# DSA attention weights left unnormalised, the outputs of a head pair multiplied by transposed reciprocals

## What is computed

```
logits = einsum('bhqd,bqkhd->bhqk', qb, kg) * D_HEAD ** -0.5     # over selected keys
logits = where(sel_ok, logits, -inf)
p = softmax(logits)                                              # exp(l - max) / sum
out = einsum('bhqk,bqkhd->bqhd', p, vg)
```

## Time and profile before

| | |
|---|---|
| median of 3 runs | 1843.07 us |
| profiled execution, own time | 1841.95 us |
| its span | 1840.2 us, mean clock of PE 0.99 |
| PE / PE loads / DVE / ACT / POOL busy, share of the span | 96% / 81% / 56% / 38% / 22% |
| DSA jobs | about 741 to 939 us from the start |
| idle of PE before an instruction, longest in the DSA stage | 4.69 us, for v_raw |

### The profile page before, as it was taken

One profiled execution on the slowest core, in us unless ns is written; L12 is line 12 of the kernel. 1 busy time (PEld: TensorE's weight loads), 2 busy tenths in 40 slices (PEclk: granted clock), 3 DMA queues, 4 the chain that ended last, 5 costly groups with the idle time before them and its releaser, 6 DMA issues. The chain is left out here.

```text
span 1840.2 us, 25612 instructions
## 1 busy us (share of the span) xinstructions
PE 1761.6 (96%) x10056; PEld 1495.7 (81%) x10056; DVE 1023.2 (56%) x1764; ACT 703.2 (38%) x1375; POOL 398.4 (22%) x174
## 2 busy tenths in 40 slices
PE   5999999999999999899999899999999999999998
PEld 4889888899877788788878688888888888888886
DVE  5387888999999997577744254323222222222225
ACT  5366444444444443799932233302111121203032
POOL 1111212321111111111014500404132222314033
PEclk9999999999999999899999899999999999999999
DMA  4564424423423323444134432302020211112023
GB/s 166 162 188 138 130 78 126 143 93 98 111 73 104 101 74 96 113 94 94 42 114 150 161 116 79 92 12 80 12 80 25 68 46 46 57 35 76 17 75 143
DMA packets 65583, 170.54 MB, mean 93 GB/s; under 512 B 9320, under 2 KB 23976, under 8 KB 65464
## 3 DMA queue, kind: packets, MB, share of 16 engines
q1 hardware_dynamic: 65464, 168.91, 30.5%
HBM read 126.47 MB, written 42.41 MB: 92 GB/s over the span
## 5 line engine op out<-in xcount | busy, mean ns | idle before, releaser
L594 PE MATMUL bk<-x_hi,w_hi 128*128 128x512 f32 (+2 forms) x832 | 308.6, 371 | 1.2 <-PEq L284 1.2
L594 PE MATMUL bk<-x_lo,w_hi 128*128 128x512 f32 (+2 forms) x832 | 298.2, 358 | 0.0
L594 PE MATMUL bk<-x_hi,w_lo 128*128 128x512 f32 (+2 forms) x832 | 297.6, 358 | 0.0
L265 POOL TENSOR_TENSOR w_lo<-w_raw,w_hi 128x1024 fp32r<-128x1024 f32 x53 | 131.4, 2480 | 478.1 <-ACT w_hi L261 478.1
L1370 ACT ACTIVATE relu<-bank 128x1024 f32<-128x1024 f32 x32 | 33.0, 1030 | 504.5 <-PE bank L1281 504.5
L1281 PE MATMUL bank<-m_hi,w_hi 128*128 128x512 f32 x512 | 199.5, 390 | 0.0
L1281 PE MATMUL bank<-m_hi,w_lo 128*128 128x512 f32 x512 | 199.2, 389 | 0.0
L1281 PE MATMUL bank<-m_lo,w_hi 128*128 128x512 f32 x512 | 199.2, 389 | 0.0
L935 DVE TENSOR_SCALAR_CACHE_REDUCE sel<-sc,st_bits 128x272 bf16<-128x272 f32 (+6 forms) x217 | 184.2, 890 | 0.9
L1451 DVE TENSOR_TENSOR acc<-acc,bank 128x1024 f32<-128x1024 f32 x56 | 68.4, 1221 | 192.5 <-PE bank L1257 191.6
L594 PEld LDWEIGHTS bk<-x_hi,w_hi 128*128 128x128 f32 x832 | 158.7, 191 | 17.0 <-issue 1.3
(11 more groups left out here) (177 smaller groups left out, 3586.9 us busy)
## 6 DMA issues: line engine op xcount, KB each, us to landing
w_raw<-w_units SPq DMA_DIRECT2D x99, 512.0 KB, 3.8
raw<-w_units SPq DMA_DIRECT2D x24, 512.0 KB, 3.5
k_hi<-k_d SPq DMA_DIRECT2D x32, 260.0 KB, 5.4
k_lo<-k_d SPq DMA_DIRECT2D x32, 260.0 KB, 6.0
q_st<-q_d SPq DMA_DIRECT2D x32, 256.0 KB, 4.6
g_d<-stage_hi SPq DMA_DIRECT2D x32, 256.0 KB
gate<-g_d SPq DMA_DIRECT2D x16, 512.0 KB, 4.4
v_raw<-v_d SPq DMA_DIRECT2D x16, 260.0 KB, 7.2
```

Source lines behind the costliest of these rows:

```text
L265: pool.tensor_tensor(w_lo[:, s], w_raw[:, s], w_hi[:, s].bitcast(F32), ALU.subtract).then_inc(lo_done, 1)
L594: mm = pe.matmul(pj[b][:, 0:c1 - c0], w[:, s, kt, :], a[:, kt, c0:c1], start=kt == 0 and k == 0, stop=kt == KT - 1 and k == 2)
```

## The change

The exponent writes its row sums to one column per job: 16 columns for the 8 blocks of a head pair. `normalise` is gone on ACT and on DVE, and `turn` of a DSA job waits for the exponent. The product is then of unnormalised weights, and ACT copies it to `o_pair` for all four pairs. When the 16 jobs of a pair have their sums, DVE inverts the 16 columns in one instruction, and ACT copies them to `r_wide`, 1024 columns, each reciprocal repeated 64 times: column block 128i + 64(head) is for block i. Eight transposes of 128x128 on PE (`turn_sums`, two groups in the ring of four banks) turn `r_wide` into the layout of `o_pair`: the partition is the head dimension of either head, the column the query. DVE multiplies the pair by the two banks (`scale_pair`), ACT rounds it, POOL makes the rest. For the last pair DVE only copies the banks to `r_last`; multiplication, rounding and rest stand at the start of the branch stage, and PE waits for them at row tile 7 of the first output tile. `sum_col`, `HI_NO` and the tile addresses are bookkeeping.

```diff
+RELOAD = [NJ // 2 + 6 + 10 * p_ for p_ in range(4)]
+PAIR_AT = [NJ // 2 + 16 * (p_ + 1) + 3 for p_ in range(3)] + [NJ + 1]
...
+    if j_ in PAIR_AT:
+        for half_ in range(2):
+            tp_take(("r", PAIR_AT.index(j_), half_), j_)
+R_GROUPS = sorted(n_ for key_, n_ in TPN.items() if key_[0] == "r")
+HI_NO = [n_ - sum(r_ < n_ for r_ in R_GROUPS) for n_ in range(len(TP_BANK))]
...
-        o_pair = at("o_pair", [P, 3, SEQ], F32, O_SC)
+        o_pair = [at(f"o_pair{p}", [P, SEQ], F32, O_SC + 4096 * p if p < 3 else O_STAGE) for p in range(4)]
+        r_wide = at("r_wide", [P, SEQ], F32, O_SC + 3 * 4096)
+        r_last = at("r_last", [P, SEQ], F32, O_STAGE + 4096)
...
+            def sum_col(j):
+                t, g, i = JOBS[j]
+                return 128 + 16 * ((g - H) // 2) + 2 * i + g % 2
...
-                    pe.wait_ge(a_done, j + 1)
+                    if t == SB:
+                        pe.wait_ge(a_done, j + 1)
+                    else:
+                        pe.wait_ge(exp_done, j + 1 - NJ // 2)
...
+                def turn_sums(p):
+                    pe.wait_ge(r_spread, p + 1)
+                    for half in range(2):
+                        n = TPN["r", p, half]
+                        turn_bank(n)
+                        for m in range(4):
+                            i = 4 * half + m
+                            mm = pe.transpose(bk[TP_BANK[n]][:, m * P:(m + 1) * P], r_wide[:, i * P:(i + 1) * P], idf[:])
                         mm.then_inc(tp_ready, 1)
...
+                    if j in PAIR_AT:
+                        turn_sums(PAIR_AT.index(j))
...
-                                   accum_out=small[:, 20 + j % 4:21 + j % 4]).then_inc(exp_done, 1)
-
-                def normalise(j):
-                    keys, s = KEYS[JOBS[j][2]], j % 2
-                    a = a_buf[:, j % 3, 0:keys]
-                    act.wait_ge(recip, j - NJ // 2 + 1)
-                    act.activation(a, a, ACT.Copy, scale=small[:, 24 + s:25 + s]).then_inc(a_done, 1)
+                                   accum_out=small[:, sum_col(j):sum_col(j) + 1]).then_inc(exp_done, 1)
...
-                    elif j < PAIRED:
-                        r = DH * (g % 2)
+                    else:
+                        r, p = DH * (g % 2), (g - H) // 2
                         if j == NJ // 2:
                             act.wait_ge(mask_done, 1)
-                        act.copy(o_pair[r:r + DH, g // 2 - 4, i * P:(i + 1) * P], bk[o_bank(j)][0:DH, 0:P]).then_inc(o_free, 1)
-                    else:
-                        r = DH * (g % 2)
-                        act.copy(o_hi[r:r + DH, g // 2, i * P:(i + 1) * P], bk[o_bank(j)][0:DH, 0:P]).then_inc(oh_done, 1)
+                        if j == NJ // 2 + 48:
+                            act.wait_ge(or_lo, 3)
+                        act.copy(o_pair[p][r:r + DH, i * P:(i + 1) * P], bk[o_bank(j)][0:DH, 0:P]).then_inc(o_free, 1)
...
+                def spread(p):
+                    if p:
+                        act.wait_ge(tp_ready, TPN["r", p - 1, 1] + 1)
+                    act.wait_ge(recip, p + 1)
+                    act.copy(r_wide[:].rearrange("p (c d) -> p c d", d=DH),
+                             small[:, 192 + 16 * p:208 + 16 * p].unsqueeze(2).broadcast_to([P, 16, DH])).then_inc(r_spread, 1)
...
                 def round_pair(p):
-                    act.wait_ge(o_free, STEPS + 16 * (p + 1))
-                    act.copy(o_hi[:, 4 + p, :], o_pair[:, p, :]).then_inc(op_hi, 1)
+                    act.wait_ge(tp_free, TPN["r", p, 1] + 1)
+                    act.copy(o_hi[:, 4 + p, :], o_pair[p][:]).then_inc(op_hi, 1)
...
-                    if 1 <= j < NJ + 1 and JOBS[j - 1][0] == DS:
-                        normalise(j - 1)
...
+                    if j > NJ // 2 and j % 16 == 0:
+                        spread((j - NJ // 2) // 16 - 1)
...
-                def normalise(j):
-                    t, g, i = JOBS[j]
-                    s, e, keys = j % 2, j - NJ // 2, KEYS[i]
-                    dve.wait_ge(exp_done, e + 1)
-                    if e >= 2:
-                        dve.wait_ge(a_done, j - 1)
-                    dve.reciprocal(small[:, 24 + s:25 + s], small[:, 20 + j % 4:21 + j % 4]).then_inc(recip, 1)
+                def reciprocals(p):
+                    dve.wait_ge(exp_done, 16 * (p + 1))
+                    dve.reciprocal(small[:, 192 + 16 * p:208 + 16 * p], small[:, 128 + 16 * p:144 + 16 * p]).then_inc(recip, 1)
...
+                def scale_pair(p):
+                    if p < 3:
+                        dve.wait_ge(o_free, NJ // 2 + 16 * (p + 1))
+                    else:
+                        dve.wait_ge(or_lo, 4)
+                    for half in range(2):
+                        n = TPN["r", p, half]
+                        src, cols = bk[TP_BANK[n]][:], slice(half * HALF, (half + 1) * HALF)
+                        dve.wait_ge(tp_ready, n + 1)
+                        if p < 3:
+                            dve.tensor_tensor(o_pair[p][:, cols], o_pair[p][:, cols], src, ALU.mult).then_inc(tp_free, 1)
+                        else:
+                            dve.tensor_copy(r_last[:, cols], src).then_inc(tp_free, 1)
...
-                def rest_output(j):
-                    t, g, i = JOBS[j]
-                    r = DH * (g % 2)
-                    dst = (slice(r, r + DH), g // 2, slice(i * P, (i + 1) * P))
-                    dve.wait_ge(oh_done, j + 1 - PAIRED)
-                    dve.tensor_tensor(o_lo[dst], bk[o_bank(j)][0:DH, 0:P], o_hi[dst].bitcast(F32), ALU.subtract).then_inc(o_free, 1)
 
...
-                    if 1 <= j < NJ + 1:
-                        if JOBS[j - 1][0] == SB:
-                            stick(j - 1)
-                        else:
-                            normalise(j - 1)
+                    if 1 <= j < NJ + 1 and JOBS[j - 1][0] == SB:
+                        stick(j - 1)
+                    if j > NJ // 2 and j % 16 == 0:
+                        reciprocals((j - NJ // 2) // 16 - 1)
                     if j < NJ and JOBS[j][0] == DS:
                         logits(j)
...
-                    if j - 4 >= PAIRED:
-                        rest_output(j - 4)
...
+                    if j in PAIR_AT:
+                        scale_pair(PAIR_AT.index(j))
...
-                        mm = unit_mm(pe, u % 2, o_hi, o_lo, outs, kts=range(4 * t, 4 * t + 4))
+                        mm = unit_mm(pe, u % 2, o_hi, o_lo, outs, kts=range(4 * t, 4 * t + 4),
+                                     before=lambda kt: pe.wait_ge(last_lo, 1) if k == 0 and kt == KT - 1 else None)
...
+                act.wait_ge(last_mul, 1)
+                act.copy(o_hi[:, KT - 1, :], o_pair[3][:]).then_inc(last_hi, 1)
...
+                dve.tensor_tensor(o_pair[3][:], o_pair[3][:], r_last[:], ALU.mult).then_inc(last_mul, 1)
+                dve.wait_ge(last_hi, 1)
+                dve.tensor_tensor(o_lo[:, KT - 1, :], o_pair[3][:], o_hi[:, KT - 1, :].bitcast(F32), ALU.subtract).then_inc(last_lo, 1)
```

More of the change, by code:

```diff
@@ L180 @@
 SEARCH[SEARCH_STEPS] = [1e8, 0.0]
-RELOAD = [STEPS + 6 + 10 * p_ for p_ in range(4)]
-PAIR_AT = [STEPS + 16 * (p_ + 1) + 3 for p_ in range(3)]
-PAIRED = STEPS + 48
 O_W = 16512
@@ L434, in build @@
             tp_ready, tp_hi, tp_free = sem("f_tp"), sem("f_tphi"), sem("f_tpfree")
-            pv_done, o_free, oh_done = sem("f_pv"), sem("f_ofree"), sem("f_oh")
+            pv_done, o_free, r_spread = sem("f_pv"), sem("f_ofree"), sem("f_rspread")
             o_spilled = [sem("f_ospill0"), sem("f_ospill1")]
@@ L571, in _ @@
                             pool.wait_ge(op_hi, p + 1)
-                            pool.tensor_tensor(o_lo[:, 4 + p, :], o_pair[:, p, :], o_hi[:, 4 + p, :].bitcast(F32), ALU.subtract).then_inc(op_lo, 1)
+                            pool.tensor_tensor(o_lo[:, 4 + p, :], o_pair[p][:], o_hi[:, 4 + p, :].bitcast(F32), ALU.subtract).then_inc(op_lo, 1)
             @block.tensor
@@ L652, in turn @@
                             mm = pe.transpose(bk[TP_BANK[n]][0:r, m * P:(m + 1) * P], a_buf[:, j % 3, c * P:c * P + r], idf[:])
+                        mm.then_inc(tp_ready, 1)
+                def turn_sums(p):
[6 more added lines that the diff above has]
+                            mm = pe.transpose(bk[TP_BANK[n]][:, m * P:(m + 1) * P], r_wide[:, i * P:(i + 1) * P], idf[:])
                         mm.then_inc(tp_ready, 1)
@@ L1010, in logits @@
                             dve.wait_ge(zd_used, z - NZ_SB)
-                        out = small[:, 16 + s:17 + s] if c1 == keys else small[:, 18 + m:19 + m]
+                        out = small[:, 16 + s:17 + s] if c1 == keys else small[:, 24 + 2 * s + m:25 + 2 * s + m]
                         dve.tensor_tensor_reduce(n_buf[:, s, c0:c1], bk[2 + z % 2][:, 0:c1 - c0], sel[:, BOFF[i] + c0:BOFF[i] + c1],
@@ L1027, in rest_weights @@
                         n, m = TPN["p", j, k], len(tiles)
-                        dve.wait_ge(tp_hi, n + 1)
```

(2 more changed lines are left out.)

## The result

The changed kernel takes 1830.3 us (median of 6 runs, 1829.36 to 1831.79) against 1842.88 (6 runs, 1841.16 to 1844.76) for the kernel before: ratio 0.9933, 95% interval 0.9924 to 0.9943. It is faster by 12.6 us; forecast was 1832.5. The profiled execution took 1829.87 (span 1828.0) where the one of before took 1841.95 (span 1840.2). The 12.1 between these are what the sum of the prediction, -10.3, has to answer for.

The account below looks back on a forecast made before the run. The prediction took ACT to bound the sparse stage, with PE next at 21.0 us a head. Its terms, -13.7 + 3.2 + 3.4 - 1.2 - 0.8 - 1.2 = -10.3 us, gave 1832.5 against the median of 1843.07, range 1824 to 1840.

Parts of the forecast that it names:

- ACT's 92%: ACT's busy share of the sparse-stage window before the change; with who waits for whom, read as ACT being the bound.
- PE's 94%: PE's busy share of the same sparse-stage window; said not to prove that PE never waits.
- Step 5: Sparse stage heads: a quarter of the 1.9 us gain per head stays as waits, 7.2 x 0.47 = +3.4 us.
- Block 7, forecast 3.05: PE's block 7 step in a sparse head: of about 1.0 us wait 0.3 stays, so 3.78 becomes 3.05 us.
- Step 3: PE in the sparse stage: 32 added transposes, 1.1 us per group of eight, three groups in the full stage, +3.2 us.
- steps 3 and 8: Three transpose groups in the full sparse stage, +3.2 us; the stage's tail, -1.2 us, with the fourth group's 1.1 in it.
- Steps 2 and 4: DVE: 64 reciprocals become four of 0.17 us each; ACT: four spreadings of 1.05, 4.2 us, 0 on the path.
- DVE as the bound (1): Rival: DVE takes ACT's place in the sparse stage, most of the gain is lost, 1840 us; chance 0.18.
- The clock (2): Rival: each transpose group or the waits around it bring a slow-clock stretch of 1.2 us, 1837.5 us; chance 0.06.
- step 6: One sparse head ran partly at half clock after a PE wait in block 7; expected away, -1.2 us.
- The weight-load share (part of 3): Rival: PE needs only 18.5 us a head by its weight loads' 81%, kernel 1808 to 1812 us; chance 0.03.
- "Slower" (4): Rival: PE already bounds the sparse stage, only the added transposes count, +4.4 us, 1847.5 us; chance 0.06.

Follow-up runs that it names:

- E4: Changed kernel with DVE again waiting each job for the previous job's exponent and inverting one unused column: 1833.43 us, ratio 0.9947.
- E5: Kernel before, with two matmuls instead of three in the sparse products (v_lo times pt_hi left out): 1843.61 us, ratio 1.0003.
- E2: Kernel before, with ACT's normalisation cut to 16 columns per job, all waits kept: 1828.69 us, ratio 0.9924.
- E3: Changed kernel with a second ACT exponent per sparse job, written to a spare tile nobody reads: 1843.75 us, ratio 1.0004.
- E6: Changed kernel with two matmuls instead of three in the sparse products (v_lo times pt_hi left out): 1816.78 us, ratio 0.9855.
- E7: Changed kernel with the third score chunk of sparse block 7 jobs issued after the step's transposes on PE: 1826.19 us, ratio 0.9908.
- E1: Changed kernel without reciprocals, spreading, their transposes and scaling, so sparse outputs stay unnormalised: 1825.1 us, ratio 0.9902.
- E12: E11 with the small write and the read issued in later steps and head 9 loaded a step earlier: 1835.65 us, ratio 0.9961.
- E11: Changed kernel with late third score chunks and loads ahead of spills, plus three pairs' reciprocals spread by DMA through DRAM: 1836.4 us, ratio 0.9958.

## Why the prediction was right, and where it was off

| Stretch | Before | After | Measured | Forecast |
| --- | --- | --- | --- | --- |
| Start of the kernel to the sparse stage's first step | 737.59 us | 737.01 us | -0.6 | 0 |
| From there to the v transposes | 21.09 us | 20.37 us | -0.7 | -0.8 |
| From there to the next block 7 | 11.44 us | 10.06 us | -1.4 | |
| Six heads from there | 138.63 us | 131.49 us | -7.1 | |
| Last head, to its block 3 step | 20.07 us | 17.96 us | -2.1 | |
| These three together | | | -10.6 | -13.7 + 3.2 + 3.4 - 1.2 = -8.3 |
| Block 3 step to the first branch product | 10.28 us | 9.17 us | -1.1 | -1.2 |
| From there to the end | 901.1 us | 902.0 us | +0.9 | 0 |
| Sum | | | -12.1 | -10.3 |

The first row is no effect of the change: nothing differs ahead of the stage (see E4). The number on record, 1832.5, has a slip: 10.3 under the median of 1843.07 is 1832.8.

**The mechanism held.** ACT set the pace of the sparse stage (E5: less PE work brings nothing; E2: less ACT time alone brings the gain; E3: its time given back takes it). With its time gone PE does (E6), down to the length of each step that the shorter copies in the earlier trace rows had shown. (Of blocks 0, 6, 5 and 4 I said that they hardly differ from head to head; block 6 took 3.56 once and block 4 2.66, waits like the others.) ACT's 92% was the right sign, PE's 94% the wrong one.

**Step 5, the residue, was sized too large.** I took 7.2 x 0.47. A head of 21.47 was expected (21.0 and a residue of 0.47) and 21.34 measured. What is left sits all in block 7, so the residue was in truth a part of the floor.

**Block 7, forecast 3.05, takes 3.34.** My sum let 0.3 of the wait of 1.0 stay. DVE starts on the first chunk only 0.73 after PE starts it, and takes 0.52:

```profile
855.84 0.52 DVE L1037 CUSTOM_DVE_ANT_0 n_buf<-bk,sel 128x348 f32<-128x348 f32 x1
```

So 0.89 lies between the second and the third chunk, where I had the issue of 0.33 and 0.3. E7 shows that this, too, can be filled. The floor was 0.3 too low and the residue 0.47 too high; that the head came within 0.13 of the forecast is luck.

**Step 3, the transposes.** 1.15 a group against 1.1. The eight span 1.16 (row 885.73), the estimate was 0.95. E1 prices the whole sum path at 5.2, where steps 3 and 8 put 4.3.

**Steps 2 and 4.** The reciprocal of 16 columns takes 0.254, near the bound of 0.3 and not the 0.17 I took; its wait is 0.9 over four. The spreading takes 1.046, as the dense copy. Both are covered. ACT's busy share of the stage is 76% and not the 70% forecast: 16.6 us a head instead of 14.8. The spreading is 0.5 of that. Another 0.7 comes from taking the 6.3 us of the normalisations off a busy time in which records overlap: without them the six heads of the trace before are busy 5.6 us a head less.

**The stage's two ends gave more than their share of heads.** At the start, the stretch at half clock behind the v_raw wait shrank from 6.8 to 3.4 us (granted clock 0.83 in 755:765, 0.70 before). At the other end I counted the last `rest_output` alone. All sixteen of them also freed PE's output banks, and in the last head of the kernel before PE waited for that in two steps, 1.06 and 0.49 us. The longer, and the one that is still there in E2, which keeps these operations and has ACT short:

```profile
919.21 0.27 PE L668 MATMUL bk<-pt_hi,v_hi 128*64 128x128 f32 x1 [1.06 <-DVE o_lo L1045]
```

```profile
912.12 0.28 PE L668 MATMUL bk<-pt_hi,v_hi 128*64 128x128 f32 x1 [0.49 <-DVE o_lo L1045]
```

These two steps took 3.70 and 3.17 and take 2.42 and 2.47, which is 2.0 of the 2.1. The experiments show whose they are. The stretch of 20.07 us takes 19.21 in E2 (`rest_output` kept, ACT short) and 17.97 both in E3 (`rest_output` gone, ACT long) and in E4 (gone, DVE's reciprocals back). So ACT's time alone would have brought 0.9, and to be without `rest_output` brings all of the 2.1 even with ACT's time back. This is wrong in kind and not only in size: a removed operation was priced by its time, and not by what its semaphore released.

**The last pair in the branch stage is hidden**, as forecast: its three operations are done at 929.6, 3.6 us after the products begin, and PE never waits for them.

**After the stage, +0.9 that no step had.** The chain that ended last, the row in which the next products begin, before and after (start, us):

```profile
1035.02 34.74 PE bank L1257 x144
```

```profile
1021.97 35.70 PE bank L1291 x144
```

The same 144 matmuls take 0.96 more. In both kernels PE waits 8.6 us ahead of them and then works at half clock (1.2 GHz) for a while; full clock (2.4 GHz) is back 3.9 us after their start before, 5.9 after. The other traces show that this is no effect of the change: all fourteen have the same wait there, the clock comes back 2.9 to 6.2 us after the start, and from the start to the end of the kernel 804.7 to 806.3 us pass, the shortest where it came back first, the longest where it came back last. What sets the moment was not tried. So up to 1.6 us of the difference between two profiled executions can be of this kind, here 0.9.

**Rivals.** DVE as the bound (1) fell: it waits for PE in the full stage, and even with its old wait given back (E4) the heads grow by 0.12 us. The clock (2): with 32 transposes more no stretch at half clock came in the full stage, and the one that was there went, as step 6 had it (1.00 in 770:914). The weight-load share (part of 3) would have had heads of 18.5; they stand at 21.34 with that share at 88%, so it was no headroom. "Slower" (4) fell with E5 and E6.

## What to carry to other kernels

A full-looking engine is told from a bound one by its own repeats: if the same step is shorter elsewhere in the trace, the engine waits in the long ones (or its clock is lower there), whatever its busy share. To test which engine sets the pace, cut work on one at a time: nothing came of 21 us of PE's before the change, 13.5 after it. When an operation goes, look who waited for its semaphore. Once an engine is the bound, even a regular wait of 0.4 us a head was worth a reordering (some 3.5 us in the stage), while moving 3.5 us of its work to small DMA elements made the kernel 12 us longer. And before a microsecond between two traces is explained, compare the stretches whose code is the same: here they differ by up to 3.9 us ahead of the sparse stage and by up to 1.6 behind it.

## What the hardware did unexpectedly

- A write of 2048 elements of 4 bytes stood before a reload in the same queue, and the reload took about 14 us to land instead of 7.5 (E12). In E11 such a write took 13.1 to 13.5 us itself, three times. Whether the queue's order or the write's own time makes the reload late was not separated.
- After the same wait of 8.6 us full clock came back anywhere from 2.9 to 6.2 us into the same matmuls, and the kernel's end followed 804.7 us after their start in the one case and 806.3 in the other.
- Reading each of 16 columns 64 times costs ACT no more than reading 1024 columns: 1.046 us against 1.048.
